# Running the first products of 56 expert chunks as a loop on TensorE, with a ring of three PSUM banks instead of four

## The chip, the cores and the metric

The kernel runs on one core of one Trainium2 chip. The metric is the device time of one execution in microseconds, the median of several runs. Lower is better. The engines are called by the names of the profile: PE (TensorE; PEld is its weight load), DVE (VectorE), ACT (ScalarE), POOL (GpSimd) and SP (SyncE, which here only issues DMAs). A q behind a name (PEq, SPq) is that engine's sequencer.

## What is computed

The reference is two transformer-like blocks over 256 tokens of width 1024. The first has gated linear attention, a spatial gating branch and a retrieval layer of single-neuron experts; the second has a SwiGLU feed-forward, differential attention beside a state-space mixer, and another feed-forward. The change touches only the retrieval layer:

```python
def block(args):
    xx, ii, gg = args
    u = expert_u[ii]
    h = jnp.einsum('tkd,td->tk', u, xx).astype(f32)
    a = (jax.nn.gelu(h) * gg).astype(x.dtype)
    return jnp.einsum('tk,tkd->td', a, expert_v[ii])
```

There are 128 x 128 = 16384 experts. Each token picks 128 of them (8 heads, 16 each) by two rankings over keys. For 160 of the 256 tokens (`TD`) the kernel computes the products with all experts densely, and gates away those that were not picked. For the other 96 tokens (`SPARSE`) it gathers the rows of the picked experts from memory.

## The kernel before, in words

**The dense part.** The experts are cut into 128 chunks of 128 experts. Two chunks are one item of 1 MB, and SP loads the items one after the other into `raw`, a ring of three slots (`RING`), by `load` (L602 to L605). A load waits until both chunks of the item before it in its slot have been used: `h_done` for the first products, `a_used` for the second products. PE waits for an item by `wait_loaded` (L540 to L543), on `slot_ready`.

For each chunk, `hidden` (L1015 to L1020) runs eight matmuls of 128x128 weights against the 160 dense tokens `XF` into a PSUM bank and counts `h_done`; each of these f32 matmuls stands in the trace as two MATMUL and two LDWEIGHTS records, so a chunk has 16 of each. ACT takes the bank, applies gelu (`early_gelu`, L1525 to L1527) into `G[:, n, :]` and counts `gelu_done`. The first 56 chunks (`FIRST`) are done by the loop at L1023 to L1028, which Python unrolls: every chunk is its own instructions. They use four banks in turn, `EARLY_BANK = (4, 5, 2, 3)`, and chunk n waits from n = 4 on until the gelu of chunk n - 4 is done:

```python
for n in range(FIRST):
    if n == 2:
        read_out(pe, "sc7")
    if n >= 4:
        pe.wait_ge(gelu_done, n - 3)
    hidden(n, ps[:, EARLY_BANK[n % 4]])
```

`read_out(pe, "sc7")` waits until ACT has copied the last score product, `sc7`, out of its bank (ACT line L1522). The score products `sc6` and `sc7` lie in banks 2 and 3; with the four banks above, chunk 2 is the first that writes bank 2 and chunk 3 the first that writes bank 3. Banks 4 and 5 have been free for longer. PE makes `sc7` at L1003, directly ahead of chunk 0.

**What runs beside it.** ACT also has, in its own order behind the gelu of chunk 11 (`n == FIRST // 5`), five copies of the rows `XROWS` (L1535, L1537), for which it waits until DVE has the list of picked rows ready (`rows_ready`, L2187), and behind the gelu of chunk 51 an exponential (L1541) with a table load on both sides. DVE ranks the scores (L2086 to L2098, L2173 to L2178), and then forms the dot products of gathered rows (`dots_to`, L2119). POOL issues the gathers (L678), each when one of six buffers is free again.

**After the 56 chunks** PE transposes the index tables (L726), and does the other 72 chunks between gate products (L1035, L1045, L1054), unrolled too, with four banks. Then come the second products of all 128 chunks (`outputs`, L1064 to L1069; `outputs_of_item`). That stage is already written as loops on PE: `pe.Fori` at L1080 with 9 turns and at L1088 with 11 turns, three items or six chunks to a turn, where `i` is a register of the sequencer and the waits on `slot_ready` are against a value that is worked out from it. It ends with a product that needs all the gathered rows (L1098, behind a wait on `row_used`), and the feed-forward of the second block follows.

Of the kernel before, what the change touches and what calls it, by code (L numbers as in the profile page):

```python
# [9 lines left out]
NT, NK = T // P, D // P  # L10
RING = 3
# [8 lines left out]
TD = T - SPARSE  # L20
ONES = 8
GROUPS = TD // ONES
FIRST = 56
# [1 line left out]
LATE = P - FIRST - BESIDE  # L25
BUFS = 6
PIECES = {(0, 0): 2, (1, 0): 3, (1, 2): 3}
EARLY_BANK = (4, 5, 2, 3)
PICKS = SPARSE
NEG = -3.0e38  # L30
FF = 2816
# [17 lines left out]
EXP0 = 2 * len(PANELS1)  # L49
# [211 lines left out]
def reads_upto(i, who):  # L261

    return sum(1 for _, e in MAIN[:i + 1] if e == who)


def program(nc, x, panels1, experts, peer_u, peer_v, ffa, panels2, ffb, cols, conv_cols, w_low, w_gate_up, w_sgu, k12,
# [4 lines left out]
    ACT = mybir.ActivationFunctionType  # L271
# [4 lines left out]
    with ctx:  # L276
# [3 lines left out]
        def sem(name):  # L280
            return ctx.enter_context(nc.semaphore(name))
# [25 lines left out]
        ps = ctx.enter_context(nc.psum_tensor("ps", [P, 8, 512], f32))  # L307
# [50 lines left out]
        G = Cut()(P, TD)  # L358
# [106 lines left out]
        h_done, gelu_done, a_used = sem("h_done"), sem("gelu_done"), sem("a_used")  # L465
# [21 lines left out]
        def read_out(eng, name):  # L487

            i = MAIN_AT[name]
            who = MAIN[i][1]  # L490
            eng.wait_ge(main_read[who], reads_upto(i, who))
# [41 lines left out]
        def half(item, h):  # L533
            return raw[:, ITEM_SLOT[item], PART * h:PART * h + PART]
# [5 lines left out]
        def wait_loaded(eng, item, more=0):  # L540

            nth = ITEM_SLOT[:item + 1].count(ITEM_SLOT[item])
            eng.wait_ge(slot_ready[ITEM_SLOT[item]], more + 16 * nth)  # L543
# [162 lines left out]
        def _(pe):  # L706
# [272 lines left out]
            for tt in range(NT):  # L979
                t = slice(P * tt, P * tt + P)  # L980
                for j in range(2, 4):
                    for q in range(2):
                        k, c = 2 * j + q, slice(512 * q, 512 * q + 512)
# [24 lines left out]
            def expert_in(n):  # L1008

                item = EXP0 + n // 2  # L1010
                if n % 2 == 0:
                    wait_loaded(pe, item)
                return half(item, n % 2)

            def hidden(n, out):  # L1015

                w = expert_in(n).rearrange("p (k e) -> p k e", k=NK)
                for k in range(NK):
                    last = pe.matmul(out[:, 0:TD], w[:, k], XF[:, k, :], start=k == 0, stop=k == NK - 1)  # L1019
                last.then_inc(h_done, 1)  # L1020

            pe.wait_ge(xf_ready, 1)
            for n in range(FIRST):  # L1023
                if n == 2:
                    read_out(pe, "sc7")
                if n >= 4:
                    pe.wait_ge(gelu_done, n - 3)
                hidden(n, ps[:, EARLY_BANK[n % 4]])  # L1028

            pe.wait_ge(sel_ready, 1)  # L1030
            transposes("idx", [s[:, tt, :] for s in (I1S, I2S, GS) for tt in range(NT)])
# [9 lines left out]
            for g in range(GROUPS):  # L1041
                for n in range(3 * g, 3 * g + 3):
                    if n >= 4:
                        pe.wait_ge(beside_done, n - 3)
                    hidden(FIRST + n, ps[:, beside_bank(n)])  # L1045
                pe.wait_ge(one_ready, g + 1)
                pe.wait_ge(one_scaled, g + 1)
                if g >= 2:
                    pe.wait_ge(gate_out, g - 1)
                    pe.wait_ge(gate_mul, g - 1)  # L1050
                gate_products(g % 2)
            for n in range(BESIDE, BESIDE + LATE):
                pe.wait_ge(beside_done, n - 3)
                hidden(FIRST + n, ps[:, beside_bank(n)])  # L1054

            pe.wait_ge(beside_done, BESIDE + LATE - 4)
            for j in range(4):
                t_claim(pe, "ffa", j)
                for q in range(2):
                    k = 2 * j + q  # L1060
# [34 lines left out]
            for j in range(4):  # L1095
                for q in range(2):
                    k = 2 * j + q
# [228 lines left out]
        def _(act):  # L1326
# [170 lines left out]
            for hf in range(2):  # L1497
                for tt in range(NT):
                    n = 2 * tt + hf
# [24 lines left out]

            def early_gelu(n):  # L1525
                act.wait_ge(h_done, n + 1)
                act.activation(G[:, n, :], ps[:, EARLY_BANK[n % 4], 0:TD], ACT.Gelu_apprx_tanh).then_inc(gelu_done, 1)  # L1527

            for n in range(FIRST):
                early_gelu(n)  # L1530
                if n == FIRST // 5:
                    act.wait_ge(xrow_ready, 1)
                    act.wait_ge(rows_ready, 1)
                    for m in (1, 2):
                        act.activation(XROWS[0:SPARSE, m, :], XROWS[0:SPARSE, 0, :], ACT.Copy)  # L1535
                    for m in range(3):
                        last = act.activation(XROWS[SPARSE:P, m, :], XROWS[32 * m:32 * m + 32, 0, :], ACT.Copy)  # L1537
                    last.then_inc(xrows_ready, 1)
                if n == FIRST - 5:
                    act.wait_ge(top_shift, 1)  # L1540
                    act.activation(GS, GS, ACT.Exp).then_inc(top_exp, 1)  # L1541
# [1177 lines left out]
```

## Time and profile before

| what | value |
|---|---|
| median of 3 runs | 1423.17 us (1422.06 to 1424.56) |
| the profiled execution, its own time | 1420.55 us |
| its span | 1418.8 us |
| PE busy | 1393.8 us (98% of the span) |
| DVE, ACT, POOL busy | 70%, 41%, 19% |
| granted TensorE clock | 0.999 |
| HBM traffic over the span | 261 GB/s |

The span runs from the first to the last instruction of the program. The profiled execution took 1.75 us more than its span, and lies 2.6 us under the median of the runs. Times in the rows are microseconds from the start of the span. "Idle before" is how long the engine had nothing to do ahead of an instruction, with what ended that; "issue" means that nothing the profile shows was waited for. Two MATMUL records on PE overlap, so that a busy PE says little; the distance from one start to the next is what a matmul costs. Some records are missing from a trace.

### The profile page before, as it was taken

The page shows a single profiled execution, that of the slowest core. Times are in us where ns is not written, and L with a number is a line of the kernel's source. Part 1 is how long each engine was busy: PE and PEld are TensorE (multiplying, and loading weights), DVE is VectorE, ACT ScalarE, POOL GpSimd, SP SyncE. Part 2 cuts the span into 40 slices and gives each one's busy share as a digit, 9 for nine tenths or more (in the row PEclk, how much of TensorE's full clock was granted, in tenths as well). Part 3 has the DMA queues.
Part 4 walks back from the last instruction along what each step waited for, and adds up shares of the span by engine and source line. Part 5 has one row for each costly group of instructions (what it writes and reads, how often), then busy time and mean ns, then how long its engine had stood idle before and what let it go on. Part 6 is the DMA issues. An engine that isn't in the chain of part 4 may idle for free.

```text
span 1418.8 us, 23437 instructions
## 1 busy us (share of the span) xinstructions
PE 1393.8 (98%) x9058; PEld 1284.5 (91%) x9058; DVE 994.2 (70%) x1816; ACT 586.4 (41%) x1114; POOL 272.5 (19%) x235
## 2 busy tenths in 40 slices
PE   8999999999999999999999999999999999999998
PEld 7788889999999999999999998888889878888886
DVE  5566746989687884544344438887889896778887
ACT  5545464311588772000000006444457585544444
POOL 1000036344265562433323310000000000000000
PEclk9999999999999999999999999999999999999999
DMA  6545545599999999999999995555554333465552
GB/s 237 179 149 178 166 149 176 200 416 405 363 384 412 408 413 370 354 417 417 416 416 417 416 390 184 198 177 192 177 173 154 120 119 118 154 215 181 194 190 89
DMA packets 67198, 371.91 MB, mean 262 GB/s; under 512 B 7969, under 2 KB 8481, under 8 KB 34866
## 3 DMA queue, kind: packets, MB, share of 16 engines
q1 hardware_dynamic: 37440, 266.45, 50.7%
q0 software_dynamic: 27648, 100.68, 17.9%
q10 hardware_dynamic: 2034, 3.76, 0.8%
q8 instruction: 48, 0.79, 0.2%
q14 instruction: 28, 0.23, 0.0%
HBM read 369.81 MB, written 1.05 MB: 261 GB/s over the span
## 4 chain that ended last, share of the span: by engine, by line
PE 87%; DVE 8%; ACT 2%; DMA 1%; issue 1%; POOL 0%; DVEq 0%; SPq 0%; ACTq 0%; POOLq 0%
PE ps L760 26%; PE ps L1019 20%; PE ps L1068 19%; PE ps L793 11%; PE ps L795 5%; PE ps L1035 3%; DVE wlo L575 2%; DVE XT L1929 1%; PE ps L792 1%; DMA raw<-in_experts 1%; PE ps L726 1%; DVE arena L2541 1%; PE ps L1241 1%; PE ps L1003 1%; ACT whi L558 0%
## 5 line engine op out<-in xcount | busy, mean ns | idle before, releaser
L1019 PE MATMUL ps<-arena,raw 128*128 128x160 f32 x2048 | 283.2, 299 | 1.2 <-DVEq L2215 1.0
L1019 PEld LDWEIGHTS ps<-arena,raw 128*128 128x128 f32 x2048 | 279.1, 190 | 2.5 <-issue 2.4
L1068 PE MATMUL ps<-arena,raw 128*128 (+1 forms) x2048 | 279.5, 299 | 0.6 <-DMA raw<-in_experts 0.4
L1068 PEld LDWEIGHTS ps<-arena,raw 128*128 128x128 f32 x2048 | 278.3, 190 | 1.6 <-issue 1.5
L558 ACT ACTIVATE whi<-raw 128x1024 fp32r<-128x1024 f32 x152 | 159.7, 1060 | 231.0 <-PE ps L760 108.7
L793 PE MATMUL ps<-XT,whi 128*128 128x512 f32 x704 | 249.6, 399 | 1.2 <-DVE wlo L575 1.0
L575 DVE TENSOR_TENSOR wlo<-raw,whi 128x1024 fp32r<-128x1024 f32 x138 | 167.1, 1221 | 70.4 <-ACT whi L558 69.6
L760 PE MATMUL ps<-whi,XT 128*128 128x512 f32 x592 | 184.7, 393 | 3.3 <-DVE XT L1929 1.5
L795 PE MATMUL ps<-XT,wlo 128*128 128x256 f32 x616 | 172.8, 281 | 0.0
L1653 ACT ACTIVATE whi<-raw 128x1024 fp32r<-128x1024 f32 x96 | 101.9, 1062 | 155.8 <-PE ps L793 101.6
L793 PEld LDWEIGHTS ps<-XT,whi 128*128 128x128 f32 x704 | 129.4, 188 | 28.4 <-DVE wlo L575 2.1
L2393 DVE TENSOR_TENSOR wlo<-raw,whi 128x1024 fp32r<-128x1024 f32 x96 | 117.2, 1221 | 44.3 <-ACT whi L1653 43.5
L760 PEld LDWEIGHTS ps<-whi,XT 128*128 128x128 f32 x592 | 109.4, 188 | 30.6 <-issue 4.7
L760 PE MATMUL ps<-XT,whi 128*128 128x256 f32 x640 | 117.2, 285 | 2.8 <-DVE wlo L575 1.1
L795 PEld LDWEIGHTS ps<-XT,wlo 128*128 128x128 f32 x616 | 116.3, 189 | 3.2
L760 PE MATMUL ps<-wlo,XT 128*128 128x512 f32 x296 | 115.4, 390 | 0.0
L2140 DVE SCALAR_TENSOR_TENSOR arena<-lo_plain,arena 128x1024 f32<-128x1024 f32 x47 | 60.4, 1284 | 73.8 <-DMA lo_plain<-in_peer_v,arena 73.5
L2140 DVE SCALAR_TENSOR_TENSOR arena<-hi_plain,arena 128x1024 f32<-128x1024 f32 x46 | 59.1, 1284 | 72.1 <-DMA hi_plain<-in_peer_v,arena 71.6
L760 PEld LDWEIGHTS ps<-XT,whi 128*128 128x128 f32 x640 | 99.4, 191 | 3.8 <-issue 1.9
L760 PE MATMUL ps<-XT,wlo 128*128 128x256 f32 x320 | 90.5, 283 | 0.0
L678 POOL DMA_INDIRECT hi_plain<-in_peer_u,arena x48 | 69.5, 1447 | 96.4 <-DVE arena L2119 67.7
L1591 ACT ACTIVATE arena<-arena 32x1024 f32<-32x1024 f32 x2 | 2.1, 1054 | 184.1 <-DVE arena L2138 184.1
(314 smaller groups left out, 1957.1 us busy)
## 6 DMA issues: line engine op xcount, KB each, us to landing
raw<-in_experts SPq DMA_DIRECT2D x128, 1024.0 KB, 7.9
raw<-in_panels SPq DMA_DIRECT2D x58, 1024.0 KB, 4.9
raw<-in_ffa SPq DMA_DIRECT2D x33, 1024.0 KB, 4.8
raw<-in_ffb SPq DMA_DIRECT2D x33, 1024.0 KB, 4.8
arena<-in_row_post ACTq DMA_DIRECT2D x4, 512.0 KB, 5.0
X<-in_x SPq DMA_DIRECT2D x2, 512.0 KB, 5.4
hi_plain<-in_peer_u,arena POOLq DMA_INDIRECT x48, 9.7
lo_plain<-in_peer_u,arena POOLq DMA_INDIRECT x48, 10.1
```

Of the source, the lines that this page charges most:

```text
L558: act.activation(whi[:, buf(p), :], half(item_of(p), p % 2), ACT.Copy).then_inc(part_hi, 1)
L575: eng.tensor_tensor(low_weights(p), half(item_of(p), p % 2), whi[:, buf(p), :].bitcast(f32), ALU.subtract).then_inc(part_lo, 1)
L678: pool.indirect_dma_start(out=GATHERED[n % BUFS], out_offset=None, in_=(peer_u, peer_v)[n // PICKS][:, :], in_offset=bass.IndirectOffsetOn ...
L760: last = pe.matmul(out, x if w_moving else w, w if w_moving else x, start=start and n == 0, stop=stop and n == 2)
L793: last = pe.matmul(out, wh[:, k], XT[:, k], start=k == 0, stop=k == NK - 1)
L795: pe.matmul(out[:, T:], wl[:, k], XTh[:, k], start=False, stop=False)
L1019: last = pe.matmul(out[:, 0:TD], w[:, k], XF[:, k, :], start=k == 0, stop=k == NK - 1)
L1035: last = pe.matmul(ps[:, 4 + 2 * b + j // 4, P * (j % 4):P * (j % 4) + P], ONE1[b][:, j, :], ONE2[:, b, j, :], start=True, stop=True)
L1068: last = pe.matmul(t_bank("ffa", k // 2)[:, at:at + TD], w[:, P * k:P * k + P], G[:, c, :], start=False, stop=False, skip_group_check=True)
L1653: act.activation(whi[:, buf(q), :], half(item_of(q), q % 2), ACT.Copy)\
L2140: ins = dve.scalar_tensor_tensor(into, v, a, into, ALU.mult, ALU.add)
L2393: dve.tensor_tensor(wlo[:, buf(q), :], half(item_of(q), q % 2), whi[:, buf(q), :].bitcast(f32), ALU.subtract).then_inc(part_lo, 1)
```

## The change

The 56 chunks are split in a first turn of six chunks, written out; eight turns of six chunks as a `pe.Fori` loop; and the last two chunks, written out. The ring of PSUM banks has three entries, (4, 5, 3), so chunk n waits for the gelu of chunk n - 3. With six chunks to a turn and three slots and three banks, each chunk of the loop's body has a fixed slot and a fixed bank in every turn; what changes with the turn are the values of the waits on `slot_ready` and `gelu_done`. The wait for the readout of `sc7` stands ahead of chunk 0; with the three banks, chunk 2 is the first that writes bank 3. In the body the wait for the item comes ahead of the wait for the gelu. ACT's gelus are written out as before, and read the three banks. The diff:

```diff
--- before.py
+++ after.py
@@ -25,7 +25,7 @@
 LATE = P - FIRST - BESIDE
 BUFS = 6
 PIECES = {(0, 0): 2, (1, 0): 3, (1, 2): 3}
-EARLY_BANK = (4, 5, 2, 3)
+EARLY_BANK = (4, 5, 3)
 PICKS = SPARSE
 NEG = -3.0e38
 FF = 2816
@@ -1014,18 +1014,31 @@
 
             def hidden(n, out):
 
-                w = expert_in(n).rearrange("p (k e) -> p k e", k=NK)
+                hidden_of(expert_in(n), out)
+
+            def hidden_of(item_half, out):
+
+                w = item_half.rearrange("p (k e) -> p k e", k=NK)
                 for k in range(NK):
                     last = pe.matmul(out[:, 0:TD], w[:, k], XF[:, k, :], start=k == 0, stop=k == NK - 1)
                 last.then_inc(h_done, 1)
 
             pe.wait_ge(xf_ready, 1)
-            for n in range(FIRST):
-                if n == 2:
-                    read_out(pe, "sc7")
-                if n >= 4:
-                    pe.wait_ge(gelu_done, n - 3)
-                hidden(n, ps[:, EARLY_BANK[n % 4]])
+            read_out(pe, "sc7")
+            turn = 2 * RING
+            for n in range(turn):
+                if n >= 3:
+                    pe.wait_ge(gelu_done, n - 2)
+                hidden(n, ps[:, EARLY_BANK[n % 3]])
+            with pe.Fori(1, FIRST // turn, 1) as i:
+                for n in range(turn):
+                    if n % 2 == 0:
+                        wait_loaded(pe, EXP0 + n // 2, i * 16)
+                    pe.wait_ge(gelu_done, (i - 1) * turn + (turn + n - 2))
+                    hidden_of(half(EXP0 + n // 2, n % 2), ps[:, EARLY_BANK[n % 3]])
+            for n in range(FIRST // turn * turn, FIRST):
+                pe.wait_ge(gelu_done, n - 2)
+                hidden(n, ps[:, EARLY_BANK[n % 3]])
 
             pe.wait_ge(sel_ready, 1)
             transposes("idx", [s[:, tt, :] for s in (I1S, I2S, GS) for tt in range(NT)])
@@ -1524,7 +1537,7 @@
 
             def early_gelu(n):
                 act.wait_ge(h_done, n + 1)
-                act.activation(G[:, n, :], ps[:, EARLY_BANK[n % 4], 0:TD], ACT.Gelu_apprx_tanh).then_inc(gelu_done, 1)
+                act.activation(G[:, n, :], ps[:, EARLY_BANK[n % 3], 0:TD], ACT.Gelu_apprx_tanh).then_inc(gelu_done, 1)
 
             for n in range(FIRST):
                 early_gelu(n)
```

## Rows read from the trace of the kernel before

**Rows 1.** The page: span, busy shares, TensorE clock in 40 slices, chain by engine.

```profile
span 1418.8 us, 23437 instructions
...
PE 1393.8 (98%) x9058; PEld 1284.5 (91%) x9058; DVE 994.2 (70%) x1816; ACT 586.4 (41%) x1114; POOL 272.5 (19%) x235
...
PE 87%; DVE 8%; ACT 2%; DMA 1%; issue 1%; POOL 0%; DVEq 0%; SPq 0%; ACTq 0%; POOLq 0%
```

**Rows 2.** The chain that ended last, by time: start us, us, what.

```profile
251.31 43.47 PE ps L1019 x320
...
585.24 113.62 PE ps L1068 x832
...
756.15 91.56 PE ps L1068 x672
```

**Rows 3.** Timeline of PE around the 56 chunks: start us, us, instruction, idle before.

```profile
251.15 123.35 PE L1019 MATMUL ps<-arena,raw 128*128 128x160 f32 x896
374.33 0.82 PE L726 MATMUL ps<-ident,arena 128*128 128x128 f32 x6
376.15 6.76 PE L1019 MATMUL ps<-arena,raw 128*128 128x160 f32 x48 [1.00 <-DVEq L2215]
```

**Rows 4.** Timeline of PE's weight loads in the 56 chunks, breaks of over 0.15 us.

```profile
251.04 43.50 PEld L1019 LDWEIGHTS ps<-arena,raw 128*128 128x128 f32 x320
294.79 4.37 PEld L1019 LDWEIGHTS ps<-arena,raw 128*128 128x128 f32 x32 [0.25 <-issue]
299.41 4.37 PEld L1019 LDWEIGHTS ps<-arena,raw 128*128 128x128 f32 x32 [0.25 <-issue]
304.10 39.31 PEld L1019 LDWEIGHTS ps<-arena,raw 128*128 128x128 f32 x288 [0.32 <-issue]
343.58 8.72 PEld L1019 LDWEIGHTS ps<-arena,raw 128*128 128x128 f32 x64 [0.17 <-issue]
352.49 21.76 PEld L1019 LDWEIGHTS ps<-arena,raw 128*128 128x128 f32 x160 [0.19 <-issue]
```

**Rows 5.** DMA from 251 to 375 us: issues, count, size, median us to landing.

```profile
raw<-in_experts SPq DMA_DIRECT2D x28, 1024.0 KB, 8.0
```

**Rows 6.** Timeline of ACT and of one weight load at the start.

```profile
249.50 0.60 ACT L1518 ACTIVATE arena<-ps 128x512 f32<-128x512 f32 x1 [5.16 <-PE ps L760]
250.39 0.60 ACT L1522 ACTIVATE arena<-ps 128x512 f32<-128x512 f32 x1 [0.30 <-PE ps L1003]
251.34 0.60 ACT L1522 ACTIVATE arena<-ps 128x512 f32<-128x512 f32 x1 [0.35 <-PE ps L1003]
251.96 1.28 ACT L1527 ACT_TABLE_LOAD   x1
...
250.15 0.19 PEld L1003 LDWEIGHTS ps<-arena 128*128 128x128 f32 x1
```

**Rows 7.** Timeline of ACT, then of DVE, around the copies behind chunk 11.

```profile
277.43 0.30 ACT L1527 ACTIVATE arena<-ps 128x160 f32<-128x160 f32 x1 [1.87 <-PE ps L1019]
277.86 2.00 ACT L1535 ACTIVATE arena<-arena 96x1024 f32<-96x1024 f32 x2
279.88 3.18 ACT L1537 ACTIVATE arena<-arena 32x1024 f32<-32x1024 f32 x3
283.08 0.50 ACT L1527 ACTIVATE arena<-ps 128x160 f32<-128x160 f32 x2
...
277.18 0.58 DVE L2187 SCALAR_TENSOR_TENSOR arena<-arena 32x32 uint32<-32x32 f32 x3
```

**Rows 8.** Timeline of ACT around the exponential behind chunk 51.

```profile
366.16 1.28 ACT L1541 ACT_TABLE_LOAD   x1
...
369.18 0.30 ACT L1527 ACTIVATE arena<-ps 128x160 f32<-128x160 f32 x1
```

**Rows 9.** The lines L1080 (loop) and L543 (slot wait): sequencer, ns min/median/max, first and last start.

```profile
L1080 PEldq COMPARE_BRANCH  x9: 76/208/234, 582.7 to 687.7; - x9
...
L543 PEldq EVENT_SEMAPHORE  x65: 51/51/51, 250.2 to 698.3; - x65
L543 PEldq ALU_OP  x20: 36/36/42, 578.3 to 840.8; - x20
```

**Rows 10.** Timeline of PE's weight loads at the start of the second products.

```profile
571.90 13.07 PEld L1068 LDWEIGHTS ps<-arena,raw 128*128 128x128 f32 x96
585.23 34.80 PEld L1068 LDWEIGHTS ps<-arena,raw 128*128 128x128 f32 x256 [0.27 <-issue]
620.21 79.89 PEld L1068 LDWEIGHTS ps<-arena,raw 128*128 128x128 f32 x587 [0.17 <-issue]
```

**Rows 11.** DMA queues of instructions, 251 to 375 us, then 572 to 690 us.

```profile
q8 instruction: 7, 0.11, 0.4%
...
q8 instruction: 1, 0.02, 0.0%
```

**Rows 12.** Windows: us, PE, PEld, DVE, ACT, POOL busy, PEclk, DMA share, GB/s.

```profile
306.00:330.00 24.00, 24.00 (x177) 23.89 (x177) 21.70 (x77) 3.34 (x11) 8.06 (x7) 1.00 1.02 416
...
375.00:400.00 25.00, 24.00 (x184) 23.88 (x183) 14.19 (x25) 22.49 (x68) 6.72 (x5) 1.00 0.84 311
```

**Rows 13.** Timeline of DVE and PE at the end of the second products.

```profile
844.10 1.28 DVE L2140 SCALAR_TENSOR_TENSOR arena<-lo_plain,arena 128x1024 f32<-128x1024 f32 x1 [0.94 <-DMA lo_plain<-in_peer_v,arena]
...
851.88 1.92 PE L1098 MATMUL ps<-arena 128*128 128x96 f32 x16
```

## The prediction

> **What bounds the kernel now.** I read the page first: PE is busy 98% of the span and makes 87% of the chain that ended last [rows 1], so a microsecond that PE loses almost anywhere is a microsecond of the total, unless something gives it back. The chain in order of time shows what PE loses in the changed stretch: 320 records take 43.47 us [rows 2], 0.1358 us from one to the next, so a chunk of 16 takes 2.17 us and the 56 chunks (896 records) 121.7 us if nothing stops them. They take from 251.15 to 374.33, 123.2 us [rows 3], so there is 1.5 us to be had in this stretch at most. The weight loads say where it lies: five breaks of 0.17 to 0.32 us [rows 4], each at an even chunk, where a new item begins. An item's slot is freed when the item before it in the slot has been used, and it is needed again four chunks later, 8.7 us; the landing takes 8.0 us in the median [rows 5], with the DMA engines full from 280 us on, at a share of 1.02 and 416 GB/s [rows 12], of which an item of 1 MB every 4.35 us is 241 and the gathers the rest. So the breaks are items that land a little late. PE's instructions themselves cost nothing here.
>
> Against the end: after the stretch PE goes on through 72 more chunks and the second products, and the last gathered row is added at 844.10 + 1.28 = 845.4, while PE needs it at 851.88 [rows 13]. PE, not the gathers, ends that part, by 6.5 us. What the change adds in the stretch is therefore handed on whole.
>
> **The change, part by part.**
>
> 1. *The wait for sc7 ahead of chunk 0.* PE used to go from sc7 straight into chunk 0, whose first weight load is at 251.04 [rows 4] and whose first matmul is at 251.15 [rows 3]. ACT copies sc7 out from 251.34 to 251.94 [rows 6]. It is now awaited, though chunks 0 and 1 write banks 4 and 5. The latency comes from the same wait one step earlier: ACT's copy of wq7 ends at 249.50 + 0.60 = 250.10, and the weight load of sc7 that waits for it starts at 250.15 [rows 6], 0.05 us later. So the first weight load comes at 251.94 + 0.05 = 251.99 if this wait is the last on the instruction, 0.95 us later than before. Behind it stands the wait for the slot, which costs a sequencer instruction of 0.05 us [rows 9], doubled to 0.1 for the step to the next, and the pipeline of loads and matmuls has to fill again, which I take at 0.05. I take **+1.1 us**, between 0.9 and 1.3. What was hidden: ACT's table load ends at 251.96 + 1.28 = 253.24 [rows 6], before chunk 0 is done in either kernel, so ACT adds nothing. An idle microsecond costs no clock either: behind a break of 1.00 us [rows 3] the granted clock stays 1.00 [rows 12].
>
> 2. *The ring of three banks.* A gelu takes 0.30 us and ACT mostly waits for PE (1.87 us before each) [rows 7], so three banks do as well as four except where ACT does other things. Twice it does. Behind chunk 11 ACT copies rows from 277.86 to 283.08 and finishes gelu 12 at 283.38 [rows 7]. Chunk 15, which now waits for it, is due at 251.15 + 15 x 2.174 = 283.76. With part 1 everything on PE is 1.1 us later, chunk 15 at 284.86. ACT is later by less: gelu 11 moves from 277.43 to 278.53, the copies start 0.2 to 0.3 us behind it at 278.8 (DVE's list, ready at 277.18 + 0.58 = 277.76 [rows 7], no longer holds them up), take 5.22 us, and gelu 12 ends at about 284.3. The margin is 0.5 us, some ten times the latency of part 1. Behind chunk 51 the table loads hold gelu 52 until 369.18 + 0.30 = 369.48 [rows 8]; chunk 55, which waits for it, is due at 251.15 + 55 x 2.174 + 1.5 = 372.2. Both waits stay covered: **0**. If the first margin were missed, the price is the miss itself; I put the bound at +0.5 us.
>
> 3. *The loop.* Each turn adds on PE's sequencer a compare-and-branch (0.21 us) and values to work out for nine waits (0.04 us each, ALU_OP) [rows 9], 0.5 us a turn. The second products have the same shape, six chunks and three items to a turn, and show what that costs. The first branch is at 582.7 [rows 9], and the turn that it leads to begins with the weight load at 585.23 [rows 10]: the sequencer is about 2.5 us ahead, more than a whole chunk, and its work hides in that. Of the eight jumps back in the first of the two loops, one coincides with a break, 0.27 us; the other break shown there, at 620.21, is not at a turn's start but four chunks into one, an item that came late [rows 10]. 832 records over nearly nine turns take 113.62 us, 0.1366 each, and 672 over seven 91.56, 0.1363 [rows 2]: against 0.1358 that is 0.6 and 0.3 us, 0.04 to 0.07 us a turn with the late items in it. For eight turns that bounds the loop at 0 to +0.6 us. I take **0**, as most jumps show no break at all.
>
> 4. *Late items inside the loop.* The lead is lost exactly when an item lands late: the sequencer stands in the wait for the slot (the EVENT_SEMAPHORE of L543 [rows 9]), and what lies between that wait and the first weight load is paid. Before, the gelu wait came first and nothing lay between. Now the gelu's value is worked out and awaited there, one ALU_OP of 0.036 us [rows 9] and the step to the next instruction, together near 0.1 us. The five long breaks [rows 4] and about two short ones (1.5 us less the 1.2 us of these) make seven: **+0.7 us**, between 0 (other items are late, or the step overlaps) and +1.2 (ten late ones, 0.12 each).
>
> 5. *Fewer instructions.* 42 of 56 chunks are no longer stored one by one. In the stretch seven 16 KB pieces of code were fetched, 0.11 MB at 0.4% of the DMA engines [rows 11]; five of them go. **0**; if all of that share reached the items, 0.4% of 8.0 us each, they would land 0.03 us earlier, -0.2 us over seven late items.
>
> The sum is 1.1 + 0 + 0 + 0.7 = **+1.8 us**, with bounds of +0.7 (0.9 - 0.2) and +3.6 (1.3 + 0.5 + 0.6 + 1.2). Made against the profiled execution, 1420.55 becomes 1422.35; the median of the runs lies 2.6 us above that execution, and the same step on it gives 1423.17 + 1.8 = **1425.0 us**. A measurement of this kernel can tell about 0.2%, 2.8 us, from no change; the forecast lies inside.
>
> At one place a rule weighs against the change. In the second products the loop fetched one 16 KB piece in 118 us, where the unrolled chunks fetched seven in 124 us [rows 11], so its body stays in PE's instruction memory from turn to turn. The Trainium skill, "Runtime: NRT & Kernel Launch", section "Instruction fetch mechanics", says that a taken branch whose target is outside the two-page window forces a fetch before execution goes on, and that kernels prefer full unrolling for that. By that rule the time is that of the third rival; the trace does not agree with it for a body of this size.
>
> **The rivals.**
>
> *Given back (no cost).* The late items depend on how the loads and the gathers meet. The gathers start when DVE's list is ready, at 277.8, whatever PE does; the loads now run 1.1 us later against them. If the late starts all fall away, 1.5 us comes back: 1.1 - 1.5 = -0.4 us, 1422.8. For it speaks that the breaks are only tenths long. Against it: the loads are issued by PE's own progress, so their budget of 8.7 us does not grow, and the DMA engines are full throughout.
>
> *The register waits take the lead away (slower).* Its place is the start of each turn and each chunk in the loop. If the sequencer can't run ahead past a wait against a register, the 0.21 us of the branch and nine ALU_OPs of 0.036 come onto PE's path, 0.53 us a turn, 4.3 us over eight turns; with part 1, 5.4 us: 1428.6. It decides once the lead at a turn's start is under 0.5 us. The second products speak against it (lead 2.5 us), but there only three waits of a turn are against registers, and here there are nine, one ahead of every chunk.
>
> *The loop fetches its body anew.* Each of the seven jumps back would wait for a load. The nearest row for a transfer in this stretch is an item, 8.0 us from issue to landing [rows 5]; less the lead of 2.5 us that is 5.5 us, 38 us in all with part 1 on top: 1463. The lower end is nothing. The body is 6 x 32 = 192 matmuls and weight loads, the same number as in the second products, where no jump costs it.
>
> **How the numbers follow.** Forecast as summed: 0.76. Given back: 0.14. Register waits: 0.08. Fetch: 0.02. The range is 1422.4 to 1428.2: from a little under the case given back to the upper bound of the sum (1426.8) and most of the way to the register case. Slower by over 0.2% (over 1426.0) are the last two rivals, 0.10, and the upper end of the sum's bounds, 0.06: 0.16. Faster by over 0.2% would need 2.8 us, more than this stretch loses; 0.02 is left for what I don't see. The rest, 0.82, is no difference.
>
> **What would show each step.** Right: the first L1019-kind weight load of the 56 chunks at about 252.0 to 252.1, idle 1 us behind an ACT release at L1522; the idx transposes (L726) at about 376.1 instead of 374.33; breaks in the weight loads only at even chunks, each 0.1 us longer than before; no break at most turn starts (chunks 12, 18, ... 48); gelu 12 done before PE asks for it, so no ACT release at chunk 15; one or two 16 KB pieces of code in the stretch instead of seven. Wrong: breaks at each turn's start or each odd chunk (register waits), breaks of some us (fetch), a break at chunk 15 or 55 (three banks), or a stage as long as before (given back). If the stage is longer by 1.8 us but the total isn't, the step from stage to end is wrong, and the place to look is the gathers at 845 us.

## The result, and the profile after

| what | before | after |
|---|---|---|
| median of 20 runs | 1422.91 us (1420.79 to 1426.71) | 1426.68 us (1424.51 to 1429.48) |
| ratio | | 1.0025, 95% interval 1.0018 to 1.0032 |
| the profiled execution, its own time | 1420.55 us | 1427.13 us |
| its span | 1418.8 us | 1425.4 us |
| granted TensorE clock | 0.999 | 0.997 |

The change makes the kernel slower by 3.8 us in the median, 0.25%. The forecast was 1425.0 us, in a range of 1422.4 to 1428.2. The ratio is not formed from the medians, so the two can differ by some 0.05%. The profiled execution of after is 6.6 us longer than that of before, more than the 3.8 us of the medians. Most of that gap comes from before: its profiled execution, 1420.55, lies 2.4 us under the median of before and under the fastest of the 20 runs, while that of after lies 0.45 us over its own median. So the sum is not to be made from these two profiles alone.

The page of the kernel after, for [rows 1]:

```profile
span 1425.4 us, 23485 instructions
...
PE 1396.0 (98%) x9058; PEld 1286.2 (90%) x9058; DVE 994.1 (70%) x1816; ACT 586.4 (41%) x1114; POOL 275.4 (19%) x235
...
PE 81%; DVE 8%; DMA 5%; ACT 3%; issue 2%; POOL 0%; SPq 0%; DVEq 0%; ACTq 0%; POOLq 0%
```

DMA has come into the chain, 5% where it had 1%. That share counts whole transfers, most of 9 to 12 us, behind waits of less than 1 us, and the same kernel in a later series (f3 below) has 5% too and lost little, so it does not say what was lost. The timeline of PE around the 56 chunks shows where, for [rows 3] (`hidden_of` is L1023 now):

```profile
252.26 34.33 PE L1023 MATMUL ps<-arena,raw 128*128 128x160 f32 x251 [0.73 <-issue]
286.91 5.19 PE L1023 MATMUL ps<-arena,raw 128*128 128x160 f32 x37 [0.32 <-issue]
294.06 14.98 PE L1023 MATMUL ps<-arena,raw 128*128 128x160 f32 x96 [1.97 <-DMA raw<-in_experts]
309.55 70.00 PE L1023 MATMUL ps<-arena,raw 128*128 128x160 f32 x512 [0.51 <-DMA raw<-in_experts]
379.39 0.82 PE L726 MATMUL ps<-ident,arena 128*128 128x128 f32 x6
```

The stretch starts 1.11 us later (252.26 against 251.15) and ends 5.06 us later (379.39 against 374.33). From 309.55 on, 512 records take 70.00 us, no more than before (70.37 for 512 in the chain of before). What was lost in the stretch lies between 286 and 310 us. Another 1.4 us are lost in the 72 chunks behind it, most of it in three places: 0.3 and 0.2 us at 458.5 and 541.9, where PE waits for DVE, which had itself waited for a gather, and 0.6 us for one late item at 561.8. The profile of f3 loses 1.4 us there too. The second products take as long as before, within 0.3 us. Windows of the part between 286 and 310 us (us, busy PE, PEld, DVE, ACT, POOL, PEclk, DMA share, GB/s):

```profile
292.00:294.00 2.00, 0.10 (x1) 0.00 (x0) 2.00 (x5) 0.30 (x1) 1.98 (x1) 1.00 0.97 410
294.00:298.20 4.20, 4.14 (x18) 4.14 (x19) 4.13 (x22) 0.10 (x1) 3.30 (x3) 0.59 1.03 428
298.20:302.00 3.80, 3.80 (x30) 3.80 (x29) 3.66 (x19) 0.51 (x2) 1.50 (x2) 1.00 1.00 408
```

PE stands still for two microseconds, and then runs at a granted clock of 0.59 in the mean of 4.2 us: 18 matmuls, where f3 below has 33 in the same window. In the trace twelve of them follow each other at 0.267 us instead of 0.136, the lower level of the clock, 1.2 GHz; that is 1.6 us more. ACT's timeline tells what came before (for [rows 7]; gelus are L1540, the copies L1548 and L1550):

```profile
278.61 0.30 ACT L1540 ACTIVATE arena<-ps 128x160 f32<-128x160 f32 x1 [1.87 <-PE ps L1023]
278.81 1.99 ACT L1548 ACTIVATE arena<-arena 96x1024 f32<-96x1024 f32 x2
280.82 3.18 ACT L1550 ACTIVATE arena<-arena 32x1024 f32<-32x1024 f32 x3
284.02 0.30 ACT L1540 ACTIVATE arena<-ps 128x160 f32<-128x160 f32 x1
286.98 0.50 ACT L1540 ACTIVATE arena<-ps 128x160 f32<-128x160 f32 x2 [2.65 <-remote]
```

The last matmul of chunk 13 starts at 282.62 in the trace and ends at 282.92, so its gelu could follow gelu 12 at once, as in [rows 7], where the two stand as one row. It starts at 286.98. SP issues the load of item 9, which waits for the same count, at 286.98 too. For the 4 us from 283 on no other engine sees a count of PE; this is called the hold-up from here on. PE itself is caught in it. Its weight loads stop inside chunk 15, after 12 of its 16, where the program has no wait:

```profile
252.23 34.26 PEld L1023 LDWEIGHTS ps<-arena,raw 128*128 128x128 f32 x252 [0.89 <-issue]
286.91 4.94 PEld L1023 LDWEIGHTS ps<-arena,raw 128*128 128x128 f32 x36 [0.43 <-issue]
```

and its sequencer works out no wait value between 282.51 and 286.94, where f3 has one at 284.90. Records of counts are missing as well: between 281 and 850 us, the time in which the gathers run, this trace holds 5122 of them, where a profile without the hold-up holds 5806 to 5842; outside that time none is missing that can be told. With item 9 not yet asked for, the gathers have the DMA engines to themselves. The DMA queues from 283.5 to 290 us (packets, MB, share of the 16 engines; q0 are the gathers, q1 the items), after:

```profile
q0 software_dynamic: 726, 2.65, 102.5%
```

and before:

```profile
q0 software_dynamic: 410, 1.49, 58.3%
q1 hardware_dynamic: 161, 1.19, 43.2%
```

Item 9 lands at 293.93, 3.9 us later than before (290.04), and chunk 18 waits for it.

### The profile page after: what moved, and what is told of

Its sections match the earlier page's. It is cut to its first block, busy times and chain, and to the rows that moved or that the text cites. A ratio compares the mean times of both kernels' runs of the same rounds, so it can differ in the third digit from the quotient of the medians.

```text
span 1425.4 us, 23485 instructions
## 1 busy us (share of the span) xinstructions
PE 1396.0 (98%) x9058; PEld 1286.2 (90%) x9058; DVE 994.1 (70%) x1816; ACT 586.4 (41%) x1114; POOL 275.4 (19%) x235
## 4 chain that ended last, share of the span: by engine, by line
PE 81%; DVE 8%; DMA 5%; ACT 3%; issue 2%; POOL 0%; SPq 0%; DVEq 0%; ACTq 0%; POOLq 0%
PE ps L760 26%; PE ps L1081 18%; PE ps L1023 16%; PE ps L793 11%; PE ps L795 5%; DMA raw<-in_experts 3%; PE ps L1048 2%; DVE wlo L575 2%; DMA hi_plain<-in_peer_u,arena 2%; DVE XT L1942 1%; PE ps L792 1%; DVE arena L2554 1%; PE ps L1254 1%; PE ps L1003 1%; ACT whi L558 0%
## 5 line engine op out<-in xcount | busy, mean ns | idle before, releaser
L1023 PE MATMUL ps<-arena,raw 128*128 128x160 f32 x2048 | 285.3, 300 | 5.2 <-DMA raw<-in_experts 2.9
L1023 PEld LDWEIGHTS ps<-arena,raw 128*128 128x128 f32 x2048 | 280.8, 191 | 7.0 <-issue 5.4
L678 POOL DMA_INDIRECT hi_plain<-in_peer_u,arena x48 | 73.0, 1522 | 91.3 <-DVE arena L2132 62.7
```

The costliest lines, as they stand in the source:

```text
L678: pool.indirect_dma_start(out=GATHERED[n % BUFS], out_offset=None, in_=(peer_u, peer_v)[n // PICKS][:, :], in_offset=bass.IndirectOffsetOn ...
```

## The experiments

Twelve experiments ran, some of them repeats of a kernel, in three series (e1 to e4; e5, e6, e7 and e0; f1 to f4). Each was timed against the kernel before in its own series: 29, 30 and 35 runs of that, with medians of 1422.24, 1422.9 and 1422.57.

**e1: the change, with the sc7 wait back at chunk 2.**

```diff
-            read_out(pe, "sc7")
             turn = 2 * RING
             for n in range(turn):
+                if n == 2:
+                    read_out(pe, "sc7")
```

> The changed kernel, but the wait for sc7 back at chunk 2. It splits the +3.8 us of the change between that wait and the rest. Theory A (the shift): the wait delays PE by 1.1 us and, by the later meeting of loads and gathers, costs about 2.5 us more; without it this run is within 1 us of the kernel before (ratio 1.000 to 1.0007). Theory B (the loop): the loop's register waits between an item's landing and its first matmul, and the three banks, cost 2.5 us by themselves; this run is 2 to 3 us over the kernel before (ratio 1.0014 to 1.002), 1.1 us under the changed kernel.

Measured: 1422.81 us, ratio 0.9999 (0.9990 to 1.0009). The loop and the three banks together have no cost that can be told from none.

**e2: the sc7 wait alone.** The kernel before, with `read_out(pe, "sc7")` ahead of its loop over the chunks.

```diff
+            read_out(pe, "sc7")
             for n in range(FIRST):
-                if n == 2:
-                    read_out(pe, "sc7")
```

> The kernel before (unrolled, four banks), with only the wait for sc7 moved ahead of chunk 0. Theory A: +3 to +4 us (ratio 1.002 to 1.0028), with items late by over 0.3 us between 285 and 310 us. Theory B: +1.1 us (ratio 1.0008), with the late items of the kernel before.

Measured: 1429.34 us in six runs, ratio 1.0046 (1.0029 to 1.0063), 7 us more than before. PE's timeline is that of the change, without loop or ring:

```profile
252.33 39.53 PE L1019 MATMUL ps<-arena,raw 128*128 128x160 f32 x288 [0.73 <-issue]
293.77 14.95 PE L1019 MATMUL ps<-arena,raw 128*128 128x160 f32 x96 [1.91 <-DMA raw<-in_experts]
```

and so are ACT's 286.88 for gelu 13 and the clock of 0.59 from 294.0 to 298.2 us. That holds up to 309 us. PE then stands idle four more times in this profile, 3.4 us in all, the longest 1.82 us for item 27, which the profile of the change does not. So the 7 us are not one cost. The wait carries the loss in this series, and the loss is more than the wait's own microsecond.

**e3: three banks alone, unrolled.**

```diff
-EARLY_BANK = (4, 5, 2, 3)
+EARLY_BANK = (4, 5, 3)
...
-                if n >= 4:
-                    pe.wait_ge(gelu_done, n - 3)
-                hidden(n, ps[:, EARLY_BANK[n % 4]])
+                if n >= 3:
+                    pe.wait_ge(gelu_done, n - 2)
+                hidden(n, ps[:, EARLY_BANK[n % 3]])
```

> The kernel before, unrolled, with only the ring cut to three banks and the sc7 wait left at chunk 2. Both theories as I hold them: no difference beyond 0.5 us, if the margin at chunk 15 holds. A third (C, the ring): without the 1.1 us of the sc7 wait PE asks for gelu 12 at 283.65, 0.27 us after ACT finishes it at 283.38, so the margin is half that of the changed kernel; if a real wait at chunk 15 costs more than its own length (the changed kernel's profile shows the sequencer stopped from 282.5 to 286.9 behind the wait of chunk 15), this run is 2 us or more over the kernel before.

Measured: 1423.33 us, ratio 1.0002 (0.9992 to 1.0012). No cost that can be told from none; theory C falls. (`early_gelu` reads the three banks as well.)

**e4: the loop alone, four banks.**

```diff
-EARLY_BANK = (4, 5, 3)
+EARLY_BANK = (4, 5, 2, 3)
...
-            turn = 2 * RING
+            turn = 4 * RING
...
-                        wait_loaded(pe, EXP0 + n // 2, i * 16)
-                    pe.wait_ge(gelu_done, (i - 1) * turn + (turn + n - 2))
+                        wait_loaded(pe, EXP0 + n // 2, i * 32)
+                    pe.wait_ge(gelu_done, (i - 1) * turn + (turn + n - 3))
```

(This diff is against the change. The sc7 wait is back at chunk 2, and the chunks outside the loop wait for the gelu four chunks back, as before.)

> The loop alone: four banks as before, twelve chunks to a turn (a first turn written out, three turns looped, eight chunks written out), sc7 wait at chunk 2. Theory A: within 1 us of the kernel before (ratio 1.000 to 1.0007). Theory B: +2 to +3 us, fewer turns but the same register waits at 36 chunks. The body is 384 matmuls and weight loads, twice that of the change: if the body has to be fetched anew when it is longer than some store, breaks of some us at the starts of chunks 24 and 36.

Measured: 1421.99 us, ratio 0.9998 (0.9989 to 1.0007). Theory B falls. The weight loads, for [rows 4]:

```profile
250.96 39.15 PEld L1023 LDWEIGHTS ps<-arena,raw 128*128 128x128 f32 x288
290.67 13.07 PEld L1023 LDWEIGHTS ps<-arena,raw 128*128 128x128 f32 x96 [0.56 <-issue]
304.41 39.15 PEld L1023 LDWEIGHTS ps<-arena,raw 128*128 128x128 f32 x288 [0.67 <-ACT arena L1541]
343.77 30.66 PEld L1023 LDWEIGHTS ps<-arena,raw 128*128 128x128 f32 x224 [0.22 <-issue]
```

The breaks come after 288, 384 and 672 records of 16 a chunk: at chunks 18, 24 and 42. Of the turn starts, 12, 24 and 36, and the loop's end, 48, only 24 is among them, and there item 12 landed late (at 304.28, first matmul at 304.42); a body of 384 matmuls and weight loads is not fetched anew.

In the profiles of e1, e3 and e4, too, no count of PE reaches ACT for a while, until 287.13 in e1:

```profile
283.53 0.50 ACT L1541 ACTIVATE arena<-ps 128x160 f32<-128x160 f32 x2
287.13 0.50 ACT L1541 ACTIVATE arena<-ps 128x160 f32<-128x160 f32 x2 [3.10 <-PE ps L1023]
```

but there chunk 13 ends ahead of it, and item 9's load goes out in time:

```profile
282.21 0.33 SPq L605 DMA_DIRECT2D raw<-in_experts  x1
```

The hold-up itself is there in all of them. Chunk 13 ends at 282.2 in e1, where its count is seen, and at 282.9 in the change, where it is not. The end of the hold-up does not move with PE: in the profiles of the change and of e1 to e4, gelu 13 or 14 starts 8.5 to 8.7 us behind POOL's first gather (278.28 in the change, 278.50 in e1). That a shift of about a microsecond decides whether item 9 is caught fits all five profiles.

**e5: e2 with the gathers 1.1 us later.**

```diff
-            pool.memset(G[:, FIRST:FIRST + BESIDE, :], 1.0).then_inc(beside_ones, 1)
+            pool.memset(G[:, FIRST:FIRST + BESIDE - 8, :], 1.0)

             pool.wait_ge(rows_ready, 1)
+            pool.memset(G[:, FIRST + BESIDE - 8:FIRST + BESIDE, :], 1.0).then_inc(beside_ones, 1)
```

> The unrolled kernel with the sc7 wait ahead of chunk 0 (e2), and the gathers started 1.1 us later (eight of the 60 chunks that POOL fills with ones are filled between the list of rows and the first gather). Loads and gathers meet as in the kernel before, both 1.1 us later. Theory A (the meeting): what is left is the 1.1 us of the wait, ratio 1.0008, between 1.000 and 1.0018. Theory D (the wait costs by itself, say by the idle microsecond on PE): as e2, ratio 1.003 to 1.005.

Measured: 1422.69 us, ratio 1.0001 (0.9987 to 1.0014). The edit moves POOL's first gather by 1.1 us (279.46, e2 has 278.35), but not the first packet of the gathers (282.80, e2 has 282.74); from 283.5 to 290 us they have 411 packets, where e6, with PE as late but the gathers not moved, has 499.

**e6: 1.1 us of idle work in place of the wait.** **e7: 4.5 us of it.**

```diff
             pe.wait_ge(xf_ready, 1)
+            keep_busy(ps[:, EARLY_BANK[0]], 5)
             for n in range(FIRST):
```

e7 has 20 in place of 5.

> The kernel before, with five idle-work matmuls (1.1 us, nobody reads them) ahead of chunk 0 and no wait moved. Theory A: the shift alone does it, as e2, +4 to +7 us. Theory D: no idle time, so +1.1 us only.

> The same with twenty such matmuls, 4.5 us, about the 4.35 us in which PE uses one item. Theory A: the loads meet the gathers as before, only one item earlier in the sequence, so the extra beyond the 4.5 us goes away: +4 to +5.5 us. If a later start is worse by its length alone, +8 us or more.

Measured: e6 1423.41 us, ratio 1.0001 (0.9992 to 1.0011); e7 1427.92 us, ratio 1.0035 (1.0021 to 1.0048), 5.0 us more for 4.5 us of work. So a shift of 1.1 us cost at most 1.6 us here, where e2 had cost 7. That spoke against theory A, if both series are alike. They are not.

**e0: the kernel before again**, in the series of e5 to e7.

> The kernel before itself, for the scatter of its profile and its time. Ratio 1.000. Open is whether its second profile also shows the stretch from 283 to 287 us in which no engine sees a count of PE (all five profiles of changed kernels show it, the first one of the kernel before doesn't). Theory A holds in both cases; if the stretch is there and items 9 and 10 of the experts are still loaded at once, chunk 13 ends ahead of it.

Measured: 1422.17 us, ratio 0.9994 (0.9985 to 1.0004). Its profile, and those of e5, e6 and e7, show no hold-up, and have their records of counts complete. The hold-up goes with the series, not with the kernel. e5 to e7 could therefore not test what happens in it, and the cure that e5 was to show stays open.

**f1 to f4** set e2, e6 and the change side by side in one series, and f4 adds e5's edit to the change.

> e2 again, beside e6 again in the same series. The profiles of e2 and e6 agree up to 282 us (gelu 11 at 278.68 and 278.70, first gather at 278.35 and 278.24), but e2's shows no count of PE arriving between 283 and 287 us and trace records lost, as all profiles of its series and of the changed kernel do, and none of e6's series does. Theory A2 (the wait's 1.1 us only matters when such a stretch follows: chunk 13 then ends inside it and item 9's load goes out 4 us late): e2 and e6 come out alike in one series, both +4 us or more with the stretch, both +0.5 to +1.5 us without. Theory D (the idle microsecond of the wait matters): e2 +4 us or more and e6 +0.5 us again.

> e6 again. Theory A2: as f1, within 1 us of it. Theory D: +0.5 us, 3 us or more under f1.

> The changed kernel in the same series. Theory A2: as f1 and f2 within 1.5 us. The loop and the ring add nothing (e1, e3, e4: -0.3 to +1.1 us).

> The changed kernel with the gathers started 1.1 us later, as in e5. Theory A2: item 9's load goes out ahead of the gathers' packets as in the kernel before, so no load goes out 4 us late: ratio 1.000 to 1.001 whatever the series. Theory D: as f3.

| run | kernel | median, us | ratio to before, 95% interval |
|---|---|---|---|
| f1 | e2: the sc7 wait alone | 1423.70 | 1.0008 (1.0000 to 1.0017) |
| f2 | e6: idle work | 1423.58 | 1.0008 (0.9998 to 1.0017) |
| f3 | the change | 1423.52 | 1.0009 (0.9999 to 1.0019) |
| f4 | the change, gathers later | 1424.48 | 1.0013 (1.0003 to 1.0023) |

The first three come out alike at +1.0 to +1.1 us, about the shift itself. So an idle microsecond costs no more than a busy one here, and theory D falls as it was put. Whether it would fall in a series with the hold-up, where e2 lost 7 us, was not tested: e6's kernel never ran in one. No profile of this series shows the hold-up. ACT's timeline in f3 has gelus 12 and 13 as one row and gelu 14 on time, and SP issues item 9 at 283.17:

```profile
284.24 0.50 ACT L1540 ACTIVATE arena<-ps 128x160 f32<-128x160 f32 x2
285.35 0.30 ACT L1540 ACTIVATE arena<-ps 128x160 f32<-128x160 f32 x1 [0.61 <-PE ps L1023]
...
283.17 0.33 SPq L605 DMA_DIRECT2D raw<-in_experts  x1
```

and PE's timeline has no long break and no slow matmuls:

```profile
252.48 52.72 PE L1023 MATMUL ps<-arena,raw 128*128 128x160 f32 x384 [0.73 <-issue]
305.40 70.41 PE L1023 MATMUL ps<-arena,raw 128*128 128x160 f32 x512 [0.21 <-DMA raw<-in_experts]
375.65 0.82 PE L726 MATMUL ps<-ident,arena 128*128 128x128 f32 x6
```

f4 gained nothing over f3 (the intervals overlap), so moving the gathers does not pay where there is no hold-up.

## Why the prediction was right, and which of its steps were not

The number was near, 1425.0 against 1426.68, and inside the range, but the measured time lies over 1426.0, in the part that was called slower and given 0.16, not in the 0.82 of no difference (the interval of the ratio reaches down to 1.0018, so it is a close call). The closeness is in part luck. Three parts of the sum held at nothing, the wait for sc7 held nearly in size, one term was mis-sized, and most of the loss in the series of the result, some 2.8 of 3.8 us, came from something that the sum does not have. The measured time lies just under the sum's upper bound, 1426.8, which was made up of costs of the ring, the loop and the late items that did not arise.

*The wait for sc7*, +1.1 us: the first matmul of the 56 chunks moved from 251.15 to 252.26, 1.11 us, but 0.2 us of that is an earlier difference of the two executions (the last matmul of sc7 starts at 251.03 and 251.25). From there to the first matmul of chunk 0 it is 0.11 us before and 1.01 in the change, e2, f1 and f3 alike; with a second step of 0.211 us in place of 0.136 the wait costs 0.97 us. The latency read from the wait one step earlier [rows 6] was the right one: ACT's copy ends at 252.16 and the first weight load starts at 252.23, 0.07 us later, so the 0.1 us for the slot wait was not paid. f1 and f3 came out +1.1 and +1.0 us in the medians, as if nothing gave it back; their intervals reach from about nothing to 2.7 us, and e5 and e6, as late on PE, came out at -0.2 and +0.5.

*Three banks*, 0: e3, 1.0002. In f3 gelu 12 starts at 284.24 and chunk 15 goes on without a break; that gelu ends at 284.54, where the forecast had it end at about 284.3. *The loop*, 0: e1 and e4, 0.9999 and 0.9998. Before, one could see this in the second products [rows 9, 10], and the changed stretch bears it out with nine register waits a turn instead of three, so the rival of the register waits falls. *Fewer instructions*, 0: from 252 to 378 us one 16 KB piece is fetched instead of seven (two in f3, four in e4), and no jump waits:

```profile
q8 instruction: 1, 0.02, 0.1%
```

so the rival of the body fetched anew falls, for bodies of 192 and 384 matmuls and weight loads. The rule of the Trainium skill ("Runtime: NRT & Kernel Launch", "Instruction fetch mechanics") does not fall with it, and the prediction applied it too widely: it speaks of a target outside a window of two pages, and counts 256 instructions to a page. The body of the change is shorter than one such page and that of e4 shorter than two, so no run here is sure to jump outside that window.

*Late items inside the loop*, +0.7 us, is the term that was mis-sized. In f3 item 12 lands at 305.27 and its first matmul starts at 305.405, 0.135 us later; in f1, which is unrolled, the numbers are 305.38 and 305.516, 0.136 us. What the loop adds is in the second step after a late start, 0.235 us instead of 0.211: 0.024 us, some 0.2 us for the forecast's seven late items (f3 has four). The sum would have been +1.2 us (0.97 and 0.2), and f3 measured +1.0.

*What the sum lacks.* In the run of the result another 2.8 us came on top (3.8 less 1.0). The sum took "a load is issued when PE has used the slot" as given. In the profile of the change and in that of e2 the count of chunk 13 arrives 4 us late; then the gathers fill the DMA engines, item 9 is 2 us late for PE, and PE's clock falls for some three microseconds. The wait for sc7 is what moves the end of chunk 13 to 282.9 us: e1 has the same hold-up and chunk 13 ahead of it, and loses nothing. e2's six runs lost 7 us in the median and the change's twenty 3.8, and the same two kernels lost 1.1 and 1.0 us in another series. Within a series the loss is no matter of a few executions: the fastest of the change's twenty took 1424.51 us, and nine of the twelve runs of f3 took less. But only one profile of each kernel and series was read, so that the hold-up is behind the loss of the other executions is inferred. *Given back*, the rival that the late starts vanish, did not happen: f3's stage still has its breaks and takes 123.17 us, as before (123.18). Its premise, that the gathers start at 277.8 whatever PE does, holds for their issue (278.05 before, 278.28 after) and not for their first packet, which came 1.1 us later (281.53 and 282.64).

What stays open: what holds PE and its counts up. It comes soon after the first packets of the gathers (282.64 in the profile of after, 281.94 in e1), but they do not time it: chunk 13's count, 0.3 us behind the first packet in both, is seen in e1 and not in after. And in the other series the packets flow without it. It goes with records that are missing just while the gathers run, so the recording itself may be part of it. And e5's edit was never run in a series with the hold-up.

## What to carry to other kernels

Put a wait where its first need is. The wait for sc7 was needed by chunk 2, the first to write that bank, and stood ahead of chunk 0, where it cost PE 1.0 us and, in one series, 3.8 us in all; in e1 the same loop with the wait at chunk 2 costs nothing. Where the bounding engine frees the buffers of a saturated DMA queue, a late start is a late order as well: compare when each load is issued with what else is about to fill the queue, and not only how long PE is busy. The loop on PE with register waits was free here because its sequencer stayed ahead, and a trace that already had such a loop showed how far ahead it was. Before a loss is put down to a kernel, compare it with a run of another kernel in the same series, and see whether the profiles have their records complete.

## What the runs showed that I had not expected

After 1.97 us without a matmul PE made four steps of the usual length and then ran at the lower level of its clock, 0.267 us a step for twelve steps, and so it did after 1.91 us in e2; both times a shorter break stood at 286 to 287 us. After 1.00 us (at 381 us in the same profile) it did not, and neither after the 1.82 us that e2 has ahead of 378.45:

```profile
378.45 2.82 PE L1019 MATMUL ps<-arena,raw 128*128 128x160 f32 x19 [1.82 <-DMA raw<-in_experts]
```

where 19 records take 2.82 us, the usual step. A wait of two microseconds for one load thus cost 3.6 us. What decides between the 1.82 and the 1.91 us isn't shown.

The same kernel measured +0.46% in one series and +0.08% in another (e2 and f1; the intervals, 1.0029 to 1.0063 and 1.0000 to 1.0017, don't overlap; the two series ran on different chips, but e5 to e7 and e0, which show no hold-up, ran on the chip of e1 to e4), beside a kernel before that stayed at 1422.2 to 1422.9 us. So a time change of a quarter of a per cent can depend on the series that it is measured in.
